# Gate slabs and MLA key/value slabs interleaved with two attentions in a two-block transformer kernel

## The reference, cut to what matters

```
# a: gated MLP mixer
u, v, g = split(rms_norm(x) @ w_in);  v = layer_norm(v)
y = u * (tril(ws) @ v + bs) * silu(g);  h = h + y @ w_out
# b: 16 heads of 64, 2 key/value heads, window of 128
q, g = split(rms_norm(h) @ w_in);  q = rotary(q + b_q)
p = softmax over band and sink (q k^T / 8);  o = p @ v
h = h + (o * silu(g)) @ w_out
# m: 8 heads, latents of rank 384 (q) and 256 (kv)
kv = rms_norm(c_kv) @ w_ukv          # per head: 128 keys, 128 values
p = softmax((qn kn^T + qr kr^T) * scale);  o = p @ v;  mix = o @ w_out
# experts: product-key top 16 of 16384, evaluated densely in u and v slabs
```

## Time and profile before

| | |
|---|---|
| median of three runs | 2379.41 us |
| the profiled execution, its span | 2376.13 us, 2374.3 us |
| TensorE busy, matmuls | 97%, 13977 |
| VectorE, ScalarE, GpSimd busy | 63%, 49%, 48% |
| mean granted TensorE clock | 0.994 of full |
| HBM read | 394 MB, 167 GB/s over the span |

### The profile page before, as it was taken

The page is one execution under the profiler, slowest core; times in us unless marked ns, Lnnn a source line. Parts: engine busy times, 40 slices in busy tenths (PEclk is TensorE's granted clock), DMA queues, the critical chain, the costliest instruction groups (busy, mean ns, idle before and its releaser), DMA issues. The chain is left out here.

```text
span 2374.3 us, 43154 instructions
## 1 busy us (share of the span) xinstructions
PE 2296.8 (97%) x13977; PEld 2045.4 (86%) x13977; DVE 1492.2 (63%) x3173; ACT 1166.0 (49%) x1775; POOL 1138.8 (48%) x493
## 2 busy tenths in 40 slices
PE   7999889999999999999999988899999999999998
PEld 5998868898999999988888877799999998888886
DVE  5433442332594888877777754429768886777777
ACT  5445434344455677743333334344557776333333
POOL 6868528576788666650000025368876667000000
PEclk9999999999999999999999999999999999999999
DMA  7544415445455444455556543245554445655653
GB/s 263 177 147 171 162 51 185 155 158 190 158 181 182 157 143 142 141 187 201 194 193 210 193 141 133 87 163 177 178 175 142 141 141 168 205 194 194 209 193 129
DMA packets 109593, 398.29 MB, mean 168 GB/s; under 512 B 12752, under 2 KB 13136, under 8 KB 108752
## 3 DMA queue, kind: packets, MB, share of 16 engines
q1 hardware_dynamic: 104688, 380.16, 47.9%
q10 hardware_dynamic: 4832, 17.17, 2.1%
HBM read 394.13 MB, written 3.15 MB: 167 GB/s over the span
## 5 line engine op out<-in xcount | busy, mean ns | idle before, releaser
L2031 POOL TENSOR_TENSOR w_lo<-ring,w_hi 128x1024 fp32r<-128x1024 f32 x474 | 1131.5, 2413 | 881.8 <-ACT w_hi L961 881.4
L961 ACT ACTIVATE w_hi<-ring 128x1024 fp32r<-128x1024 f32 x722 | 743.0, 1056 | 542.1 <-PE XX L435 389.4
L433 PE MATMUL GG<-hT_both,w_hi 128*128 128x256 f32 x1728 | 490.5, 284 | 3.4 <-POOL w_lo L2031 2.2
L434 PE MATMUL GG<-hT_both,w_hi 128*128 128x256 f32 x1728 | 488.9, 283 | 0.0
L435 PE MATMUL GG<-hT_both,w_lo 128*128 128x256 f32 x1728 | 488.9, 283 | 0.0
L543 PE MATMUL GG<-hT_both,w_hi 128*128 128x512 f32 x1152 | 410.4, 399 | 0.1
L433 PE MATMUL XX<-w_hi,hT_both 128*128 128x512 f32 x1024 | 398.8, 389 | 2.7 <-DVE w_lo L1897 2.1
L434 PE MATMUL XX<-w_lo,hT_both 128*128 128x512 f32 x1024 | 398.4, 389 | 0.0
L435 PE MATMUL XX<-w_hi,hT_both 128*128 128x512 f32 x1024 | 398.4, 389 | 0.0
L1897 DVE TENSOR_TENSOR w_lo<-ring,w_hi 128x1024 fp32r<-128x1024 f32 x248 | 303.9, 1225 | 56.1 <-ACT w_hi L961 56.0
L433 PEld LDWEIGHTS GG<-hT_both,w_hi 128*128 128x128 f32 x1728 | 331.5, 192 | 5.1 <-POOL w_lo L2031 2.6
(11 more groups left out here) (296 smaller groups left out, 2729.8 us busy)
## 6 DMA issues: line engine op xcount, KB each, us to landing
ring<-slabs_in SPq DMA_DIRECT2D x722, 512.0 KB, 4.0
big<-rows_in ACTq DMA_DIRECT2D x10, 512.0 KB, 7.0
big<-rows_in ACTq DMA_DIRECT2D x3, 1024.0 KB, 9.0
big<-keys_in ACTq DMA_DIRECT2D x2, 1024.0 KB, 7.6
h_kept<-h ACTq DMA_DIRECT2D x2, 1024.0 KB, 10.8
h<-h_kept ACTq DMA_DIRECT2D x2, 1024.0 KB, 6.7
big<-ws_in ACTq DMA_DIRECT2D x1, 1024.0 KB, 14.6
out<-h SPq DMA_DIRECT2D x4, 256.0 KB, 2.0
```

Of the source, the lines that this page charges most:

```text
L433: nc.tensor.matmul(out, a_hi, b_hi, start=start, stop=False, skip_group_check=True)
L434: nc.tensor.matmul(out, a_hi, b_lo, start=False, stop=False, skip_group_check=True)
L961: nc.scalar.activation(w_hi[:, 2 * j + half, :], ring[j][:, half * 1024:(half + 1) * 1024], ACT.Copy).then_inc(hi_ready, 1)
L2031: Q.tensor_tensor(w_lo[:, 2 * j + half, :], ring[j][:, half * 1024:(half + 1) * 1024], w_hi[:, 2 * j + half, :], ALU.subtract).then_inc(sp ...
```

## The change

Four things are changed; all results stay what they were.

1. Start: filler matmuls before and after the first transposition; ScalarE rounds block 0 right after the first half slab; VectorE writes block 0's lo part before it finishes the norm of block 1. The mask of `A_ws` is eight instructions of two groups each, one after each of the `a_u` slabs 8 to 15; the band mask follows them.
2. First attention: only gate slab 0 is multiplied ahead. The 24 pieces (6 matmuls each) of gate slabs 1 to 3 go between the units: four around the last q transposition, then two ahead of each of the transpositions 0 to 9. Value products come at units 9, 10 and 11, in the order 0, 2, 1, 3; `b_out` begins once the two halves that its first slab needs are gated. In that stretch ScalarE rounds six half slabs between its units, and VectorE, not GpSimd, writes their lo parts. ScalarE's silu of slabs 1 to 3 follows its last exponential.
3. MLA start: 13 fillers go into a G bank, free since long.
4. MLA attention: keys and values of heads 4 to 7 are multiplied ahead of transpositions 0 to 3; 9 fillers ahead of `m_kv`, not 12.

```diff
-PV_AFTER = {"b": [1, 3, 7, 11], "m": [1, 3, 5, 7]}
+VALUES_OF = {"b": [range(0, 2), range(2, 4), range(4, 8), range(8, 12)], "m": [range(2 * i, 2 * i + 2) for i in range(4)]}
+VALUES_AT = {"b": {9: [0], 10: [2], 11: [1, 3]}, "m": {2: [0], 4: [1], 6: [2], 7: [3]}}
     for k in range(n):
+        if name == "m" and k < 4:
+            out.append(("k", k))
         out.append(("t", k))
...
                     if kind == "t":
+                        if between is not None:
+                            between(k)
                         pe.wait_ge(sem(f"p_{name}"), k + 1)
...
             pe.wait_ge(sem("ident_ready"), 2)
+            busy_at_start(22)
             transpose_block("a_tr", xs, "xs_a", 0)
+            busy_at_start(13)
...
-            project_cols("b_g", hT, DC)
+            project_slab(SLAB0["b_g"], 0, hT, DC, False)
+            def gate_chunk(n):
+                s, c = SLAB0["b_g"] + 1 + n // DC, n % DC
+                half = c // 4
+                if c == 0:
+                    bank_free(s, 0)
+                q = half_ready(s, 0, half)
+                for a in range(2):
+                    last = triple(G[s % 4][:, a * T:(a + 1) * T], ..., c == 0 and a == 0, c == DC - 1)
+                if c % 4 == 3:
+                    last.then_inc(half_done, 1)
+            def gate_chunks(k):
+                for n in range(4 + 2 * k, min(6 + 2 * k, 3 * DC)):
+                    gate_chunk(n)
...
-            transpose_rows("b_qtr", B_q)
+            transpose_rows("b_qtr", B_q, tiles=(0, 1, 2))
+            gate_chunk(0)
+            gate_chunk(1)
+            transpose_rows("b_qtr", B_q, tiles=(3,))
+            gate_chunk(2)
+            gate_chunk(3)
...
-            attention("b", b_scores, b_transposes, b_values)
-            pe.wait_ge(sem("b_y_ready"), 4)
-            project_wide("b_out", (B_yh, B_yl))
+            attention("b", b_scores, b_transposes, b_values, gate_chunks)
+            project_wide("b_out", (B_yh, B_yl), sem("b_y_ready"), needed=lambda p, half: 2 * p + 2)
...
-            busy_until("m_tr", 2, 14)
+            bank_free(SLAB0["m_in"], 0)
+            keep_busy(G[SLAB0["m_in"] % 4], 13)
...
 # ScalarE
             root_block("a", 0)
             split_half(0, 0)
-            root_block("a", 1)
-            split_half(0, 1)
             act.wait_ge(sem("cols_loaded"), 16)
             round_block("a_tr", hT_hi, 0, "a_g")
+            split_half(0, 1)
+            root_block("a", 1)
...
+            attention("b", True, DH ** -0.5, then={
+                ("t", 0): lambda: split_half(SLAB0["b_g"] + 3, 0), ("t", 1): lambda: split_half(SLAB0["b_g"] + 3, 1),
+                ("t", 3): lambda: split_half(SLAB0["b_out"], 0), ("t", 5): lambda: split_half(SLAB0["b_out"], 1),
+                ("t", 7): lambda: split_half(SLAB0["b_out"] + 1, 0), ("s", 11): lambda: take_gates([1, 2]),
+                ("t", 9): last_gates})
 # VectorE
+                if b == 1:
+                    dve.wait_ge(sem("cols_loaded"), 16)
+                    rest_block("a_tr", *hT, 0, "a_g")
                 inverse_root("a", b)
...
-            attention("b", True, DH ** -0.5, b_unit, b_gated)
+            attention("b", True, DH ** -0.5, b_unit, b_gated, {10: [0], 11: [2, 1, 3]}, {
+                2: lambda: rest_half(SLAB0["b_g"] + 3, 0), 3: lambda: rest_half(SLAB0["b_g"] + 3, 1),
+                5: lambda: rest_half(SLAB0["b_out"], 0), 7: lambda: rest_half(SLAB0["b_out"], 1),
+                9: lambda: rest_half(SLAB0["b_out"] + 1, 0), 11: lambda: rest_half(SLAB0["b_out"] + 1, 1)})
 # GpSimd
-            Q.affine_select(out=A_ws, in_=A_ws, compare_op=ALU.is_ge, fill=0.0, base=0,
-                            pattern=[[0, 16], [1, P]], channel_multiplier=-1).then_inc(sem("ws_masked"), 1)
+            for q in range(8):
+                split(8 + q, 9 + q)
+                two = A_ws[:, 2 * q:2 * q + 2, :]
+                Q.affine_select(out=two, in_=two, compare_op=ALU.is_ge, fill=0.0, base=0,
+                                pattern=[[0, 2], [1, P]], channel_multiplier=-1).then_inc(sem("ws_masked"), 1)
```

More of the change, by code:

```diff
@@ L61, in attention_order @@
     for k in range(n):
+        if name == "m" and k < 4:
+            out.append(("k", k))
         out.append(("t", k))
-        while values < len(PV_AFTER[name]) and (PV_AFTER[name][values] < k or k == n - 1):
-            out.append(("v", values))
-            values += 1
+        out += [("v", i) for i in VALUES_AT[name].get(k, [])]
         if k + AHEAD < n:
@@ L447, in wide_half, with project_wide @@
                 return last
-            def project_wide(stage, src, ready=None, first=0):
+            def project_wide(stage, src, ready=None, first=0, needed=lambda p, half: 2 * p + half + 1):
                 per, groups = WIDE[stage], SLABS[stage] // WIDE[stage]
@@ L455, in inputs_ready @@
                     if ready is not None:
[L456 removed]
+                        pe.wait_ge(ready, needed(p, half))
                 for g in range(first, groups):
@@ L602, in busy_until, with attention @@
                 keep_busy(x_begin(stage, i), n)
-            def attention(name, scores, transposes, values):
+            def attention(name, scores, transposes, values, between=None):
                 for kind, k in attention_order(name):
@@ L607, in attention @@
                     if kind == "t":
+                        if between is not None:
+                            between(k)
                         pe.wait_ge(sem(f"p_{name}"), k + 1)
                     if kind == "v":
-                        first = PV_AFTER[name][k - 1] + 1 if k else 0
-                        for u in range(first, PV_AFTER[name][k] + 1):
+                        for u in VALUES_OF[name][k]:
                             x_read(pe, f"{name}_t{u}")
+                    if kind == "k":
+                        if k % 2 == 0:
+                            half_ready(SLAB0["m_kv"] + 1, 0, k // 2)
+                        keys_values(4 + k, x_begin(stage, 0))
+                        if k % 2:
+                            half_used(stage, 0)
+                        continue
+                    if (kind, name) == ("s", "m") and k >= 4:
+                        x_read(pe, f"m_k{k - 4}")
                     tile = x_begin(stage, 0)
@@ L1181, in _, with take_gates, last_gates @@
             take_T("b_qtr", B_qT)
-            attention("b", True, DH ** -0.5)
+            def take_gates(slabs):
+                for j in slabs:
+                    tile, free = g_tile(act, "b_g", j, j)
+                    nc.scalar.activation(flat(B_gT)[:, j * 512:(j + 1) * 512], tile[:, :], ACT.Silu).then_inc(free, 1)
+            def last_gates():
+                take_gates([3])
+                split_half(SLAB0["b_out"] + 1, 1)
+            attention("b", True, DH ** -0.5, then={
[3 more added lines that the diff above has]
+                ("t", 9): last_gates})
             seam("b_out", "fin", "r_v", lambda: round_block("r_tr", hT_hi, 0))
```

109 lines of the change are left out of this document (64 added, 45 removed).

## The result

The kernel after took 2340.89 us (median of 4 runs, 2340.52 to 2341.27), the kernel before 2379.18 (median of 4, 2378.58 to 2382.72): ratio 0.9836, 95% interval 0.9819 to 0.9853. A second set of runs gave 2340.35 against 2378.65, again 38.3 us less. The forecast was 2340.5. So the two profiles lie 35.6 us apart (35.5 in the span). The first product of one and the same start came between 13.1 and 14.4 us in nine profiled executions, so a difference of a microsecond between two profiles means little by itself.

The account below looks back on a forecast made before the run. TensorE was taken as the bound, with gains from its waits, slow clock and fillers. 3.8 + 2.2 + 23.9 + 8.0 + 1.0 = 38.9 from 2376.1 gives 2337.2; median 3.3 higher, 2340.5; range 2333 to 2354.

Parts of the forecast that it names:

- The first attention: From gate slab 0 to `b_out`: gate work fills waits, 50.4 us in all, gain 23.9; ends 14 and 26.
- The start of MLA: Fillers run without their 6.0 us wait, the product begins at 1399.1, not 1407.5: gain 8.0; ends 6 and 8.4.
- The start: First products: earlier by 2.2 us and at full clock, less GpSimd waits: gain 3.8; ends 0 and 6.
- The two waits of 0.9 for GpSimd: At the start: TensorE waits some 0.9 and 0.9 us for the first and last of GpSimd's rests.
- the products' better clock: At the start: 12 matmuls at 0.23 in place of 0.42 us give 2.3 more.
- The masks: GpSimd's 4.3 us of masks leave the path, TensorE waited 2.2 for it: gain 2.2; ends 1 and 2.7.
- The spatial product behind them: Band mask ahead of the spatial product shifts GpSimd's halves by under a microsecond: -0.5 to +0.8, taken as 0.
- Keys and values: MLA: four heads moved into the attention cover waits ahead of transpositions 0 and 3: gain 1.0; ends -1.5 and 1.8.
- The landings: Rival: slab landings set the start, start gain 0; 35 in all, 2344 us; chance 0.12.
- VectorE did not take over: Rival: VectorE takes over the first attention, gain there 14, 29 in all, 2350 us; chance 0.11.
- The pieces: Rival: pieces don't move into the first attention's waits; only later parts gain, 15 in all, 2364 us; chance 0.04.
- The half clock did not stay: Slower rival: half clock stays through the interleaved first attention, which loses 25; total 2389 us; chance 0.03.

Follow-up runs that it names:

- e1: The kernel before with only the first attention and its gate pieces changed; start, masks, MLA start, keys and values as before: 2353.53 us.
- e4: The kernel before with 43 filler matmuls in the waits of its first attention, none of the change: 2375.92 us.
- e5: The kernel after, with the six halves of weights in the first attention split by GpSimd, not VectorE: 2345.75 us.
- e3: The kernel after with the start of MLA as before, 14 fillers in the X bank again: 2348.47 us.
- e2: The kernel after without the fillers and the new order of the start; masks stay in pieces: 2343.36 us.
- e7: The kernel after without the 35 filler products at the start; the new order of the first roundings stays: 2341.26 us.
- e6: The kernel after with MLA's keys and values of all eight heads multiplied ahead of the second attention: 2340.70 us.
- e8: The kernel after, unchanged, run again with a second profile: 2340.35 us.
- e9: The kernel after, with VectorE adding the latent rest to MLA's value products one normalization later: 2334.34 us.
- e10: The kernel after, with VectorE rotating MLA's query tile before it normalizes the latent keys: 2336.75 us.
- e11: The kernel after with both edits, e9's and e10's: 2331.24 us.
- e12: The kernel after, with the output projection behind the first attention waiting for all four gated tiles: 2342.36 us.

## Why the prediction was right, step by step

**The first attention** (23.9 predicted): 24.4 in the profiles, 25.1 in e1's runs. Its parts: 50.4 us predicted and 50.03 measured; a unit 3.0 and 2.96; waits of 0.6 and 0.6 against 0.61 for the normalization and 0.49 for the k tile's bank. The step that could have failed, that VectorE's unit and a half of weights fit into TensorE's unit, held: one wait in front of a transposition is left of 12 in that attention (17 less MLA's 5). The estimate of 4 to 5 us for the half clock was high: e4 has 3.2. What the prediction did not see is why VectorE had to do it: e5's 5.4 us. The change of function table was visible and hidden (1.28 us, the next instruction at once, as before).

**The start of MLA** (8.0): 8.3 in the profiles, 8.1 in e3.

**The start** (3.8): 3.2 in the profiles, 3.0 in e2's median. The first product at 13.24 was forecast as 13.2; that it fits to 0.04 is luck, since other executions of the same start have it as late as 14.38. The two waits of 0.9 for GpSimd were 0.47 and 0.20, and later ones of 0.52 and 1.02 (at 42.95 us; 0.21 and 0.89 before) were not in the sum. Nor was the 0.70 us for the second half of the second transposition: the prediction has VectorE and GpSimd exclude each other in the spatial product, and did not see that its own new order puts VectorE's normalization of block 1 beside GpSimd's halves (4.84 us for 0.88). I let the products' better clock count with 2.3 us; e7 leaves at most 0.9 of it, so this part of the term was mis-sized, and most of the gain is the order's.

**The masks** (2.2): 2.2 in the profiles. No run takes the masks alone. By medians, the parts that e1 leaves out are worth 13.2 us, and e2, e3 and e6 have 11.5 of them, which leaves 1.7 with an error as large as e2's. The spatial product behind them (0, from -0.5 to +0.8): its first wait is 0.5 us longer (1.25 for 0.75), but by gate slab 0 the loss is made up (-5.4 to -5.5).

**Keys and values** (1.0): 1.1, if the second half clock in that stretch is counted as 1.6 (+0.5 in the table). e6's runs can't tell it from 0.

**The sum.** The terms came to 38.9; measured are 39.2 (3.2 + 2.2 + 0.1 + 24.4 + 8.3, with 1.1 less the 0.1 at the queries' slab). Two things had no term. The kernel after has two half clocks in MLA that before's profiled execution did not have, +1.5 at the queries and +1.6 in the attention, and 0.5 in small change: 2337.2 was forecast for the profiled execution and 2340.5 measured. And the 3.3 us by which the median stood above the profiled execution belonged to that one execution: for the kernel after they are 0.4. These two are of equal size and opposite sign, so the forecast of the median met to 0.4 us, better than it had earned: that closeness is luck. Both probably have one cause: executions differ in which of the waits has a half clock behind it (the table below), and before's profiled one had few. The runs of before agree with that: in the three sets, the ten with a mean granted clock of 0.991 or 0.992 took 2379.47 to 2382.32 us, and the nineteen with 0.993 or 0.994 took 2376.26 to 2379.76.

**The rivals.** The landings did not set the start (3.0 and not 0; all four runs of e2 are slower than e8's four). VectorE did not take over. The pieces did move into the waits. The half clock did not stay through the interleaved attention: 1.00 in that stretch in e1, e5, e8 and the kernel after.

## What to carry to other kernels

Look for dense work that an engine can do inside a stretch of short dependent steps before you make the steps faster: here 17.3 us of products went into a stretch that was 70% busy, and it became 7 us shorter. Price each engine's share of the new order by its rows in the state it will have then: in these rows work on VectorE is cheap where GpSimd is quiet and dear where it is not, and a new order can move an instruction from the one place to the other. In an order written by hand, ask at each wait whether the engine that ends it stood idle behind something that nobody wanted yet: two such swaps gave 9.1 us here.

## What the runs showed of the hardware

**VectorE beside GpSimd.** An instruction that reads SBUF operands can be held for the length of a whole instruction of GpSimd: 2.30 against 0.23 us for a product of 64 columns, up to 2.47 against 0.36 for a normalization, 4.84 against 0.88 for the two at the start. The products of the query tile's rotation, which have an operand in PSUM, kept their 0.42. The Trainium skill (SBUF — State Buffer, Who interferes with whom) says that two SBUF inputs, or one in a fast mode that uses both ports, contend with GpSimd and that the second to issue blocks until the first is done. The rows of the product with two SBUF inputs agree; in which mode the normalizations ran no row shows.

**Half clocks.** The granted clock falls to 1.2 GHz for 3.4 us (sometimes 6.8) near certain waits, but not near each one in every execution. One of 3.4 us costs 1.6 to 1.7 us, half of what TensorE works in it (3.30 to 3.42 us). Where they stood in the one profiled execution of each kernel, between 20 us and the end of the experts:

| kernel | half clock at (us) |
|---|---|
| before | 277, 318 (6.8 long), 1397 (10.2 long), 1503 |
| after | 1405, 1460, 1467 |
| after, again (e8) | 1407, 1465 (6.8 long) |
| e1 | 67, 1374 (6.8 long), 1419, 1480 |
| e2 | 44, 122, 1413, 1471 (6.8 long) |
| e3 | 1367 (10.2 long), 1466, 1473 |
| e4 | 68, 123, 1396 (10.2 long), 1502 |
| e5 | 1410, 1465, 1472 |
| e6 | 1408, 1462, 1469 |
| e7 | 117 (6.8 long), 1462, 1469 |
| e9 | 118 |
| e10 | 1461 (6.8 long) |
| e11 | none |
| e12 | 1461, 1468 |

The same wait can be followed by one or not. The wait of 2.5 to 2.6 us for the query tile's bank has a half clock right behind it in six of the twelve executions that have the wait. The pair of waits of 0.6 to 1.2 and 0.86 us in MLA's attention has one in six of twelve, and the wait of 1.6 us in the spatial product has one beside it in four of fourteen. The wait of 2.2 us ahead of MLA's last transposition has one in all twelve, but a wait as long at the end of the first attention (2.17 us in e5, 2.16 in e12) has none. What decides in a given execution stays open. The spread of a kernel's runs doesn't follow the number in its profile: the kernel after, with two or three, has the closest (0.62 us in e8), e11 has 0.96 and e2 5.4.
